# The RWKV stage of a two-block network: features and read-out placed anew between the masked copies

## The reference

```python
k = xk @ wk
v = heads(xv @ wv)
kk = heads(k * k_k)
kk = kk * lax.rsqrt(jnp.maximum(jnp.sum(kk * kk, axis=-1, keepdims=True), 1e-24))
for d in range(2):
    w_raw = heads(w0[d] + jnp.tanh(xw @ w1[d]) @ w2[d])
    decay = jnp.exp(-jnp.exp(-jax.nn.softplus(-w_raw) - 0.5))
    a = jax.nn.sigmoid(heads(a0[d] + (xa @ a1[d]) @ a2[d]))
    k_d = kh * (1 + (a - 1) * k_a_h)
# the recurrence, for each direction
S = (S * w_t - einsum('bhij,bhj->bhi', S, kk_t)[..., None] * kka_t + v_t[..., None] * k_t)
y = einsum('bhij,bhj->bhi', S, r_t)
# the read-out
yn = (y - mean) * rsqrt(var + GN_EPS) * ln_g + ln_b
bonus = sum(r * k_sum * r_k) * v
out = ((yn + bonus) * g) @ wo
```

## Time and profile before

| | us |
|---|---|
| median of 3 runs (lowest, highest) | 4855.08 (4850.23, 4858.95) |
| the profiled execution, its own time | 4856.1 |
| its span in the trace | 4854.3 |
| TensorE busy in the span | 4618.8 (95%) |
| VectorE busy | 2698.2 (56%) |
| ScalarE busy | 1038.9 (21%) |

### The profile page before, as it was taken

The page is one execution under the profiler, slowest core; times in us unless marked ns, Lnnn a source line. Parts: engine busy times, 40 slices in busy tenths (PEclk is TensorE's granted clock), DMA queues, the critical chain, the costliest instruction groups (busy, mean ns, idle before and its releaser), DMA issues.

```text
span 4854.3 us, 70234 instructions
## 1 busy us (share of the span) xinstructions
PE 4618.8 (95%) x29914; PEld 3264.4 (67%) x29914; DVE 2698.2 (56%) x4820; ACT 1038.9 (21%) x2331; POOL 81.2 (2%) x81
## 2 busy tenths in 40 slices
PE   7999999998998998899999999989999999989998
PEld 5556555555546666674888688644888788645886
DVE  3172445535336666663565666674656666674656
ACT  1052000002026555652000210042001110152000
POOL 0000000000000000000000000020000000020000
PEclk9998999998999899998999999989999999989999
DMA  5211122211100000012222222211222222211221
GB/s 235 104 45 52 58 107 113 118 74 44 73 1 2 3 3 3 2 38 78 87 87 87 73 87 83 97 55 53 87 87 78 87 87 78 87 53 70 87 87 44
DMA packets 27046, 339.09 MB, mean 70 GB/s; under 512 B 3025, under 2 KB 3025, under 8 KB 6897
## 3 DMA queue, kind: packets, MB, share of 16 engines
q1 hardware_dynamic: 24048, 324.51, 17.8%
q0 software_dynamic: 2688, 10.09, 0.6%
HBM read 330.40 MB, written 4.19 MB: 69 GB/s over the span
## 4 chain that ended last, share of the span: by engine, by line
PE 87%; DVE 7%; ACT 3%; issue 2%; DMA 0%; SPq 0%; DVEq 0%; ACTq 0%
PE ps L1359 45%; PE ps L1077 23%; PE ps L1558 2%; PE ps L1149 2%; PE ps L1530 2%; PE ps L1489 1%; PE ps L1606 1%; PE ps L1119 1%; PE ps L1541 1%; PE ps L1614 1%; ACT arena L1799 1%; PE ps L1300 1%; PE ps L1427 1%; PE ps L1479 1%; PE ps L1575 1%
## 5 line engine op out<-in xcount | busy, mean ns | idle before, releaser
L1359 PE MATMUL ps<-arena 128*128 128x256 f32 (+1 forms) x9096 | 2112.5, 394 | 15.1 <-DVE arena L2625 15.1
L1359 PEld LDWEIGHTS ps<-arena 128*128 128x128 f32 x9096 | 1731.9, 191 | 383.4 <-DVE arena L2625 17.5
L1077 PE MATMUL ps<-arena 128*128 128x512 f32 (+3 forms) x3104 | 1153.2, 532 | 10.7 <-ACT arena L1750 7.4
L1077 PEld LDWEIGHTS ps<-arena 128*128 128x128 f32 x3104 | 584.3, 192 | 567.5 <-issue 401.5
L2616 DVE TENSOR_TENSOR arena<-ps,arena 128x512 f32<-128x512 f32 (+1 forms) x250 | 157.6, 630 | 315.5 <-PE ps L1359 313.7
L2616 DVE TENSOR_TENSOR square<-ps,square 128x512 f32<-128x512 f32 (+1 forms) x145 | 99.2, 684 | 176.3 <-PE ps L1359 176.3
L2557 DVE TENSOR_TENSOR arena<-arena 128x1024 f32<-128x1024 f32 (+2 forms) x153 | 190.5, 1245 | 8.7 <-ACT arena L1750 5.4
L1940 ACT COPY square<-ps 128x512 f32<-128x512 f32 (+1 forms) x65 | 37.2, 573 | 659.4 <-PE ps L1359 592.4
L1558 PE MATMUL ps<-arena 64*64 64x64 f32 x3072 | 131.5, 229 | 13.0 <-ACT arena L2013 12.3
L1940 ACT COPY arena<-ps 128x384 f32<-128x384 f32 (+1 forms) x35 | 18.5, 530 | 575.1 <-PE ps L1359 549.2
L2031 ACT COPY arena<-ps 128x256 f32<-128x256 f32 x240 | 88.4, 372 | 233.3 <-PE ps L1530 232.8
(11 more groups left out here) (341 smaller groups left out, 4897.4 us busy)
## 6 DMA issues: line engine op xcount, KB each, us to landing
arena<-in_panels SPq DMA_DIRECT2D x144, 2048.0 KB, 7.8
arena<-in_panels SPq DMA_DIRECT2D x9, 1536.0 KB, 6.4
arena<-in_bias POOLq DMA_DIRECT2D x8, 512.0 KB, 4.6
arena<-in_x_in SPq DMA_DIRECT2D x1, 3072.0 KB, 11.0
x_save<-arena POOLq DMA_DIRECT2D x1, 2048.0 KB, 7.5
arena<-x_save POOLq DMA_DIRECT2D x1, 2048.0 KB, 12.9
out_x<-arena SPq DMA_DIRECT2D x8, 256.0 KB, 2.2
arena<-in_panels SPq DMA_DIRECT2D x1, 1792.0 KB, 11.6
```

What stands on the lines that cost most here:

```text
L1077: ins = pe.matmul(dest, left(k), right(k), start=(k == 0), stop=(k == nk - 1))
L1359: ins = pe.matmul(bank[:, j * cut.side:(j + 1) * cut.side], left[:, k, j * P:(j + 1) * P], right[k], start=(k == 0), stop=(k == cut.rows - 1))
```

## The change

The tables are written anew, and nothing that is computed changes. The key norm's square, norm and root leave A: they are issued in C of the pair before, at steps 12, 14 and 15 (`NORM_AHEAD`), and for pair 1 ahead of the loop. In A the reciprocals are spread from step 0 to 7, "kk" goes from 11 to 9, and two of the six "run" go to B. "exp" of direction 0 goes from A, step 15, to B, step 7. "key" and "rate" of direction 0 go from B's steps 1 and 2 to 3 and 4. The three "kr" of direction 0 and "exp" of direction 1 go from B to C (steps 0, 1 and 2), those of direction 1 from C's steps 3 to 5 to 6 and 7, its "key" and "rate" from 1 and 2 to 3 and 4, "k_sum" from 6 to 8, and "bonus" from 7 to 14. In the read-out the Square gets a step of its own (3, "squares"), "var" goes from 6 to 5, "root" from 7 to 6, and the reciprocals from 8-11 to 7-10.

```diff
         FEATURES = (
-            {1: [("square", 0, 0)], 3: [("norm", 0, 0)], 4: [("root", 0, 0)], 5: [("recip", 0, 0), ("lora", 0, 0)],
-             6: [("recip", 0, 1), ("lora", 1, 0)], 7: [("recip", 0, 2)], 8: [("recip", 0, 3), ("run", 0, 0)],
-             9: [("recip", 0, 4), ("run", 0, 1)], 10: [("recip", 0, 5), ("run", 0, 2)], 11: [("kk", 0, 0)],
-             12: [("run", 1, 0)], 13: [("lora", 0, 1), ("run", 1, 1)], 14: [("lora", 1, 1), ("run", 1, 2)], 15: [("exp", 0, 0)]},
-            {1: [("rate_k", 0, 0), ("key", 0, 0)], 2: [("rate_k", 1, 0), ("rate", 0, 0)], 3: [("kr", 0, 0)], 4: [("kr", 0, 1)],
-             5: [("kr", 0, 2)], 6: [("exp", 1, 0)]},
-            {1: [("key", 1, 0)], 2: [("rate", 1, 0)], 3: [("kr", 1, 0)], 4: [("kr", 1, 1)], 5: [("kr", 1, 2)],
-             6: [("k_sum", 0, 0)], 7: [("bonus", 0, 0)], 9: [("bk", 0, 0)], 10: [("bk", 0, 1)], 12: [("bk", 1, 0)],
-             13: [("bk", 1, 1)]})
+            {0: [("recip", 0, 0)], 1: [("recip", 0, 1)], 3: [("recip", 0, 2)], 4: [("recip", 0, 3)], 5: [("lora", 0, 0)],
+             6: [("recip", 0, 4), ("lora", 1, 0)], 7: [("recip", 0, 5)], 9: [("kk", 0, 0)], 10: [("run", 0, 0)],
+             12: [("run", 0, 1)], 13: [("lora", 0, 1), ("run", 0, 2)], 14: [("lora", 1, 1), ("run", 1, 0)]},
+            {0: [("run", 1, 1)], 1: [("rate_k", 0, 0)], 2: [("rate_k", 1, 0), ("run", 1, 2)], 3: [("key", 0, 0)],
+             4: [("rate", 0, 0)], 7: [("exp", 0, 0)]},
+            {0: [("kr", 0, 0)], 1: [("kr", 0, 1), ("kr", 0, 2)], 2: [("exp", 1, 0)], 3: [("key", 1, 0)], 4: [("rate", 1, 0)],
+             6: [("kr", 1, 0)], 7: [("kr", 1, 1), ("kr", 1, 2)], 8: [("k_sum", 0, 0)], 9: [("bk", 0, 0)], 10: [("bk", 0, 1)],
+             12: [("bk", 1, 0)], 13: [("bk", 1, 1)], 14: [("bonus", 0, 0)]})
+        NORM_AHEAD = {12: "square", 14: "norm", 15: "root"}
...
-        READOUT = {1: "centre", 6: "var", 7: "root", 8: "recip0", 9: "recip1", 10: "recip2",
-                   11: "recip3", 12: "scale", 13: "shift", 14: "gate"}
+        READOUT = {1: "centre", 3: "squares", 5: "var", 6: "root", 7: "recip0", 8: "recip1", 9: "recip2",
+                   10: "recip3", 12: "scale", 13: "shift", 14: "gate"}
...
             for step in LATE:
                 e["feature"](0, *step)
+            for what in NORM_AHEAD.values():
+                e["feature"](1, what, 0, 0)
...
+                    if t % GROUPS == 2 and k in NORM_AHEAD and t // GROUPS + 2 < PAIRS:
+                        e["feature"](t // GROUPS + 2, NORM_AHEAD[k], 0, 0)
...
-                elif what == "var":
+                elif what == "squares":
                     act.wait_ge(sem("ro_centred"), p + 1)
```

## The result

The changed kernel takes **4822.6 us** (median of four runs, 4821.2 to 4823.4) against 4856.5 for the kernel before (four runs, 4850.2 to 4859.0). The ratio is 0.993, with a 95% interval of 0.992 to 0.994: 34 us faster, where 39 were forecast. The profiled execution took 4823.4.

What follows compares the result with a forecast made beforehand. Each gap was taken to last as long as its slowest engine link, VectorE in A's gap 4, ScalarE in B's gap 3. Terms -50 - 5 + 1 - 0.7 + 13 + 1 + 2 gave -39 us: 4816 us, range 4798 to 4842.

Steps and rivals of the forecast that it cites:

- A: First third of a pair in the RWKV stage: 36.4 to 29.3 us, 7 times, so 50 us less.
- C: Last third of a pair: 2.2 us more in 6 pairs (13 us), 1 in the seventh; gap 5 critical.
- B: Middle third of a pair: 0.8 us less in each of 6 pairs, 5 us in all.
- what would show it: Signs in the stage: masked-copy waits from 22 us to a few, A 29 to 30, C about 28.
- rival 1: Clock stays low in A: gain there 35 us, C perhaps 5 dearer; 4836 us, chance 0.17.
- Rival 4: No change, as ScalarE and not VectorE bounds all gaps of A: 4853 us, chance 0.07.
- rival 3: Slower, as the loss moves into C, 10.6 us more in 6 pairs: 4865 us, chance 0.06.
- rival 2: Clock stays up in B too, giving 3 us each, and C costs 0.8 less: 4799 us, chance 0.14.
- "0.7 more" less "0.8": B's gap 1: run ahead of the state's clearing, 0.7 us more; read-out's centring no longer behind key, 0.8 less.
- the first B: The B with features alone: 1 us more, by the run and the new table load.
- The last B: The B with the read-out alone: 0.7 us less.
- Ahead of the loop: Norm of pair 1 between bonus and the first masked copy: 2 us more (0 to 4).

## Why the prediction was right, point by point

The size was right, and two of its three large terms were right to a few per cent. The third, B, had the wrong sign, and the term of C came out right from a working that names the wrong engine, which is luck.

**What bounded the kernel: right.** VectorE held A's gap 4, ScalarE B's gap 3. Moving 1.4 us of VectorE's work out of gap 4 alone shortened it by 1.17; moving the norm alone left it at 5.75. The waits for the masked copy fell from 22.2 to 5.9 us, as "what would show it" asked.

**A: right, gap by gap.** Forecast were 4.9, 6.4, 4.2, 4.9 and 2.15 us for gaps 2 to 6, and the trace has 5.05, 6.28, 4.08, 5.15 and 1.96: 29.31 in all against 29.3. The clock of gaps 5 and 6 is 1.00, so rival 1 fell in A, and the kernel with two scans moved showed that less waiting of TensorE in gap 4 was enough. Rival 4 fell with gap 4 at 4.08, rival 3 with C at 28.0 and a clock of 1.00, rival 2 with B's clock of 0.85. Over its eight thirds A gave 51 us (280.0 to 228.6), where 50 were in the sum.

**B: mis-sized, by about 9 us.** The sum had -5 + 1 - 0.7 and the trace has +4.6 (260.8 to 265.4 over the eight thirds). The six in the middle gave nothing (207.3 to 207.4) where 5 were put. The failing terms:
- gap 3, "6.9 against 9.11": it takes 7.7, and the mean of the six pairs before was 8.8, so it gave 1.1 and not 2.2. ScalarE's busy time (6.47 for 6.5) and TensorE's wait at its end (2.68 for 2.7) were right. What was short is the tail. I had put 0.4 from the end of the chain's last copy to the masked copy, and it takes 1.02, all of it at the lower clock. The chain, and then the tail as a stretch:

```profile
1750.74 1.28 ACT L2090 ACT_TABLE_LOAD   x1
...
1753.35 1.28 ACT L2075 ACT_TABLE_LOAD   x1
1754.65 0.84 ACT L2075 ACTIVATE arena<-arena 128x768 f32<-128x768 f32 x1
...
1756.13 0.62 ACT L2017 COPY arena<-ps 128x256 f32<-128x256 f32 x2
1756.53 1.12 PE L1562 MATMUL ps<-arena 64*64 64x64 f32 x16 [2.68 <-ACT arena L2017]
```

```profile
1756.75:1757.77 1.02, 1.02 (x24) 1.02 (x23) 0.00 (x1) 0.00 (x1) 0.00 (x0) 0.50 0.00 0
```

- gap 1, "0.7 more" less "0.8": it takes 11.3 at a clock of 0.85 in four of six pairs where about 10.4 were put. The 0.7 for the run was right (0.6 at full clock). What the sum left out is that the clock could fall in this gap: 1.5 us.
- gap 2, "5.2", takes 4.7, which gives 0.5 of it back.
- the first B, features alone, grew by 3.7 (24.7 to 28.4) where 1 was put. 2.1 of this is its gap 3, where the Exps now come with a load and TensorE idles 2.75 us for 1.23. The last B grew by 0.8 where 0.7 less was put. In the second trace of the same kernel it fell by 0.5 (28.3), with its gap 4 at a clock of 1.00 instead of 0.64, so this miss is the clock.

**C: right in size, wrong in its link.** 28.0 were forecast (25.8 + 2.2) and 28.03 came, with gap 5 at 6.41 against 6.4. C's eight thirds grew by 13.9 in all (208.6 to 222.4), against 14. But the working named VectorE's queue, with "bonus" ahead of the norm's read and the bank that this read frees, and had the norm's matmuls "fit in the wait" with 0.9 us. In the changed kernel this is how it stands, the gap first:

```profile
1788.43:1794.84 6.41, 6.31 (x106) 4.05 (x106) 5.19 (x10) 5.66 (x13) 0.00 (x0) 1.00 0.01 3
...
1791.37 1.56 PE L1625 MATMUL ps<-square,const 128*128 128x384 f32 x4
1791.42 0.74 DVE L2973 SCALAR_TENSOR_TENSOR arena<-arena,vec 128x512 f32<-128x512 f32 x1
1792.32 1.20 DVE L2930 TENSOR_SCALAR rstd<-ps 128x384 f32<-128x384 f32 x2 [0.16 <-PE ps L1625]
...
1793.03 1.10 PE L1640 MATMUL ps<-arena,const 128*128 128x512 f32 x2
1794.23 0.69 DVE L2997 TENSOR_TENSOR reset<-reset,ps 128x512 f32<-128x512 f32 x1 [0.71 <-PE ps L1640]
```

The norm's read waits for its matmul even here, by 0.16, so "bonus" was covered, and taking it away only made the wait 0.82. The bank costs next to nothing either: the read-out's matmul starts at 1793.03, 0.1 us after the norm's matmuls end. There is no wait for them to fit in. TensorE was busy in all of this gap before (4.77 of 4.77 us) and is busy for 6.31 of 6.41 now; the norm's four matmuls take 1.56, and with the 0.1 they are the whole 1.6. The norm's first read ends at nearly the same time (1792.9), so this trace alone can't tell TensorE's queue from the bank. Two runs can. With only the norm moved, "bonus" was not in this gap, and it took 6.40 too. With turn and bonus of the read-out early, no matmul stands behind that bank there, and gaps 4 and 5 together are only 0.2 shorter. So TensorE's own work carries the cost of C's gap 5, and that the working by VectorE's queue gave the same 1.6 is chance. The root on ScalarE is hidden, as put: gap 6 of C stays 2.08.

**Ahead of the loop: right.** I had put 2 us. In the kernel before the first masked copy starts 0.66 us after "bonus" does, right behind it (1435.57 and 1436.23). In the changed kernel it is 2.88 (from 1433.57):

```profile
1436.45 0.44 DVE L2863 COPY_PREDICATED arena<-const,ps 128x256 f32<-128x256 int32 x1 [1.20 <-ACT arena L2001]
```

These 2.2 us don't show in the start of the stage (1436.2 and 1436.4) only because everything ahead of it came 2 us earlier in this trace; the second trace of the same kernel starts the stage at 1437.9.

**The table loads.** The sum had the six new loads at 1.28 us each and nothing behind them. In the changed kernel's rows above the load at 1753.35 ends at 1754.63 and the Exp starts at 1754.65. The Trainium skill, page "ScalarE: Activation LUTs", section "What ACT_TABLE_LOAD costs", gives the same load and a drain of 1380 ns more; no row here shows that drain. Its section "Table sets: the hidden batching unit" has the rule to batch activation calls by set. In this kernel the number of loads doesn't order the times: three loads a pair took 4842 to 4858 us, four took 4818 to 4844, and five took 4794 to 4818, depending on where "exp" and its load stood.

## What to carry to other kernels

In a ring over several engines price a filler by the engine that has no idle time in that gap. 1.56 us of TensorE's work in a gap that TensorE fills cost 1.6, and 2.95 us of ScalarE's work in a gap with room for it cost nothing. Where a filler makes TensorE wait, add what the clock may cost: 0.68 us of VectorE's work ahead of a small clearing cost 0.6 at full clock and 2.1 where the clock fell. When a step leaves a gap, look at the gap that it enters, and at the ones behind it for TensorE's clock; of the change's 7 us in A the 1.7 of gap 6 only changed places. Undoing one move at a time finds such a step, and here the version with the run back in A and "exp" at B's step 0 beats the change by 26 us.
